# Silu on ScalarE in place of a sigmoid and a product on VectorE, in a two-layer decoder trunk

## The reference

```python
def swiglu(h, w_gate_up, w_down):
    g, u = jnp.split(h @ w_gate_up, 2, axis=-1)
    return (jax.nn.silu(g) * u) @ w_down
# layer 0:  h = h + swiglu(rms_norm(h), ffn_w_gate_up, ffn_w_down)
# layer 1:  out = sum over e of gates[:, e] * swiglu(hn, w_gate_up[e], w_down[e])
```

## Time and profile before

| | before |
|---|---|
| runs | 1892.37, 1892.75, 1894.83 us |
| median | 1892.75 us |
| profiled execution, its span | 1892.9 us |
| TensorE busy | 1694.2 us (90%) |
| VectorE busy | 1352.8 us (71%), 1387 instructions |
| ScalarE busy | 1084.9 us (57%), 1089 instructions |
| mean granted TensorE clock | 0.948 of full speed |
| dense mixer, first activation | 267.87 us after the start |
| ends of the eight turns (last products) | 894.7 to 1831.2 us |

### The profile page before, as it was taken

One profiled execution on the slowest core, in us unless ns is written; L12 is line 12 of the kernel. 1 busy time (PEld: TensorE's weight loads), 2 busy tenths in 40 slices (PEclk: granted clock), 3 DMA queues, 4 the chain that ended last, 5 costly groups with the idle time before them and its releaser, 6 DMA issues.

```text
span 1892.9 us, 21567 instructions
## 1 busy us (share of the span) xinstructions
PE 1694.2 (90%) x7672; PEld 1384.0 (73%) x7672; DVE 1352.8 (71%) x1387; ACT 1084.9 (57%) x1089; POOL 0.2 (0%) x4
## 2 busy tenths in 40 slices
PE   6998889997878686799899999998998998999986
PEld 5885768885658565688787787786886886877865
DVE  6645444555438363798898897897997987988964
ACT  5354333344434342676676676675776766766753
POOL 0000000000000000000000000000000000000000
PEclk9999889998888796899999999999999999999998
DMA  5552334553425104599798897897896996987922
GB/s 223 215 181 86 134 113 177 200 184 127 141 101 185 54 25 187 213 373 347 280 368 316 316 374 306 306 378 285 332 375 255 367 377 244 369 337 293 373 109 89
DMA packets 64077, 459.62 MB, mean 243 GB/s; under 512 B 7200, under 2 KB 7200, under 8 KB 8480
## 3 DMA queue, kind: packets, MB, share of 16 engines
q1 hardware_dynamic: 64032, 459.01, 64.5%
HBM read 457.94 MB, written 1.05 MB: 242 GB/s over the span
## 4 chain that ended last, share of the span: by engine, by line
PE 79%; DVE 11%; ACT 5%; issue 3%; DMA 1%; DVEq 0%; ACTq 0%; SPq 0%
PE banks L366 25%; PE banks L368 24%; PE banks L367 24%; DVE weights_low L1062 3%; ACT weights_high L744 2%; PE banks L439 2%; PE banks L414 1%; DMA raw_static<-static_dram 1%; PE banks L691 1%; PE banks L690 1%; DVE activations_t L1084 1%; DVE residual L1497 1%; ACT activations_t L770 1%; DVE scores_t L1385 0%; PE banks L609 0%
## 5 line engine op out<-in xcount | busy, mean ns | idle before, releaser
L1062 DVE TENSOR_TENSOR weights_low<-scratch,weights_high 128x2048 fp32r<-128x2048 f32 x336 | 761.5, 2289 | 114.8 <-ACT weights_high L744 114.7
L744 ACT ACTIVATE weights_high<-scratch 128x2048 fp32r<-128x2048 f32 x336 | 642.6, 1915 | 124.5 <-PE banks L368 124.4
L366 PE MATMUL banks<-weights_high,activations_t 128*128 128x512 f32 (+1 forms) x1568 | 628.3, 401 | 66.0 <-DVE weights_low L1062 49.8
L367 PE MATMUL banks<-weights_low,activations_t 128*128 128x512 f32 (+1 forms) x1568 | 614.2, 392 | 0.0
L368 PE MATMUL banks<-weights_high,activations_t 128*128 128x512 f32 (+1 forms) x1568 | 614.2, 392 | 0.0
L366 PEld LDWEIGHTS banks<-weights_high,activations_t 128*128 128x128 f32 x1568 | 301.7, 192 | 130.8 <-DVE weights_low L1062 32.4
L368 PEld LDWEIGHTS banks<-weights_high,activations_t 128*128 128x128 f32 x1568 | 301.3, 192 | 62.1
L367 PEld LDWEIGHTS banks<-weights_low,activations_t 128*128 128x128 f32 x1568 | 302.4, 193 | 56.6
L1062 DVE TENSOR_TENSOR weights_low<-raw_static,weights_high 128x2048 fp32r<-128x2048 f32 x99 | 221.8, 2257 | 123.3 <-ACT weights_high L744 121.8
L744 ACT ACTIVATE weights_high<-raw_static 128x2048 fp32r<-128x2048 f32 x99 | 185.1, 1892 | 122.6 <-PE banks L368 110.2
L366 PE MATMUL banks<-weights_high,hidden_t 128*128 128x512 f32 x536 | 214.3, 400 | 9.5 <-DVE hidden_t L1236 9.5
(11 more groups left out here) (226 smaller groups left out, 1026.2 us busy)
## 6 DMA issues: line engine op xcount, KB each, us to landing
scratch<-expert_dram SPq DMA_DIRECT2D x336, 1024.0 KB, 5.5
raw_static<-static_dram SPq DMA_DIRECT2D x97, 1024.0 KB, 4.9
consts_sb<-const_dram SPq DMA_DIRECT2D x1, 1058.0 KB, 6.9
residual<-x_dram SPq DMA_DIRECT2D x1, 1024.0 KB, 4.9
out_dram<-residual SPq DMA_DIRECT2D x2, 512.0 KB, 2.8
small_sb<-small_dram SPq DMA_DIRECT2D x1, 704.0 KB, 8.1
raw_static<-static_dram SPq DMA_DIRECT2D x2, 256.0 KB, 3.0
scratch<-gain_dram SPq DMA_DIRECT2D x1, 512.0 KB, 5.7
```

The costliest lines, as they stand in the source:

```text
L366: pe.matmul(oo, xh, wh, start=first, stop=False)
L367: pe.matmul(oo, xh, wl, start=False, stop=False)
L744: A(WH[:, slot, 0:w], raw[:, 0:w], ACT.Copy).then_inc(high_ready, 1)
L1062: V_.tensor_tensor(WL[:, slot, 0:w], raw[:, 0:w], WH[:, slot, 0:w].bitcast(F32), ALU.subtract).then_inc(low_ready, 1)
```

## The change

In `f_sigmoid` ScalarE evaluates Silu in place of Sigmoid. In `f_hidden` VectorE's first product, the one with the gate columns, is gone together with the wait behind it; the product with the up columns reads `SIG`, which now holds silu(g). The helper `elink` and the semaphore `hid_step` go too, since nothing else uses them. `link` stays for other uses. The name of the function `f_sigmoid` and of its semaphore stay. No slab, bank, DMA or order of other work is touched.

```diff
-        dve_step, hid_step = sem("dve_step"), sem("hid_step")
+        dve_step = sem("dve_step")
...
                 for tt in range(tiles):
-                    m = A(SIG[:, tt, :], gu_bank(n, tt)[:, 0:256], ACT.Sigmoid)
+                    m = A(SIG[:, tt, :], gu_bank(n, tt)[:, 0:256], ACT.Silu)
                 m.then_inc(f_sig, 1)
...
-            def f_hidden(n, fbase, tiles, gu_bank, linked):
+            def f_hidden(n, fbase, tiles, gu_bank):

                 dve.wait_ge(f_sig, fbase + (n + 1))
-                for tt in range(tiles):
-                    m = V_.tensor_tensor(SIG[:, tt, :], SIG[:, tt, :], gu_bank(n, tt)[:, 0:256], ALU.mult)
-                linked(m)
                 for tt in range(tiles):
                     m = V_.tensor_tensor(HID[:, tt, :], SIG[:, tt, :], gu_bank(n, tt)[:, 256:512], ALU.mult)
                 m.then_inc(f_hid, 1)
...
-                f_hidden(n, 0, NT, lambda n, tt: PS[:, 6 + tt, :], link)
+                f_hidden(n, 0, NT, lambda n, tt: PS[:, 6 + tt, :])
...
-                lk = [0]
-
-                def elink(m):
-                    lk[0] += 1
-                    m.then_inc(hid_step, 1)
-                    dve.wait_ge(hid_step, it * ESTEPS + lk[0])
-
...
-                    f_hidden(n, it * ESTEPS + FSTEPS, 1, lambda n, tt: PS[:, 2 + n % 2, :], elink)
+                    f_hidden(n, it * ESTEPS + FSTEPS, 1, lambda n, tt: PS[:, 2 + n % 2, :])
```

## The result

| | before | changed |
|---|---|---|
| runs beside the prediction, median | 1892.56 us (1892.06 to 1894.83, 4) | 1881.98 us (1880.04 to 1884.12, 4) |
| ratio to before | | 0.9937 (0.992 to 0.9954) |
| all unedited executions on record, mean | 1893.7 us (60) | 1882.5 us (13) |
| mean granted clock, where recorded | 0.9483 (56) | 0.9525 (13) |
| profiled execution, its span | 1892.9 us | 1878.5 us |

The change made the kernel 10.6 us faster by the first medians and 11.2 by the means, where 6.7 were forecast. The executions of either kernel scatter over several us (1878.5 to 1885.4 for the changed one), so a pair of profiles is not a measurement: these two differ by 14.4 us.

The account below looks back on a forecast made before the run. TensorE was taken as the bound, busy for 90% of the span, with VectorE's products mattering only where TensorE waits for them. Terms 3.5 + 0.8 + 1.6 + 0.8 = 6.7 us off 1892.75 gave 1886.1 us, range 1882.5 to 1890.5.

Parts of the forecast that it names:

- the clock at the turns' heads: Head of an expert turn: the one clock fall in seven may vanish or move; 0.8 us gained, half of 1.6.
- the stretch behind the dense mixer: From the dense mixer to the experts: the prediction's sum had no term for it, so no gain.
- Turn ends: End of each of eight expert turns: the remaining product starts 0.44 us sooner and all of it counts; 3.5 us gained.
- Dense first step: First dense mixer step: the exposed wait before the second step shrinks from 2.32 to 1.53 us; 0.79 us gained.
- The clock behind the dense stall: Behind the dense mixer's first-step stall: the shorter stall should mostly pass without a clock fall; 1.6 us gained.
- Silu, table loads, the freed time in the steps: Activations and mid-turn steps: Silu takes 385 ns like the sigmoid, table loads stay as many, VectorE's other freed time gains 0.
- slower by the clock: Rival, heads of turns: the 2.08 us stall costs a clock fall in all seven turns; 1898.1 us, chance 0.05.
- more clock than that: Rival, expert turns: two or three of the eight falls behind 2.88 us stalls may vanish too; 1881 to 1883 us, chance 0.10.
- Direct terms only: Rival, whole kernel: clock falls stay as many, only 4.3 us are gained; 1888.4 us, chance 0.20.
- nothing is gained: Rival, turn ends: something arriving no sooner holds the transposes or the next turn's first slab; 1892 us, chance 0.12.
- the two slower ones: Rivals: clock falls at all seven heads, 1898.1 us, chance 0.05; extra table loads in each step, some 1960 us, chance 0.02.

Follow-up runs that it names:

- e3: Changed kernel with a second, serial product back in the last step of each expert only; 1889.0 us, ratio 0.9973 to the kernel before.
- e6: Changed kernel with a second, serial product back in all steps of an expert but the last; 1882.0 us, ratio 0.9932 to the kernel before.
- e2: Kernel before with the change made in the experts only, the dense mixer keeping sigmoid and two products; 1887.31 us, ratio 0.9967.
- e4: Changed kernel with the second pair of products back in the first dense step only; 1886.39 us, ratio 0.9957 to the kernel before.
- e1: Kernel before with the change made in the dense mixer only, the experts keeping sigmoid and two products; 1888.53 us, ratio 0.9978.
- e5: Changed kernel with the second pair of products back in the ten later dense steps; 1884.18 us, ratio 0.9948 to the kernel before.
- e7: Changed kernel with a one-column Silu ahead of the expert loop, loading its table there; 1874.25 us, ratio 0.9901 to the kernel before.
- e0: Changed kernel again, unedited, for more executions; 1882.74 us, ratio 0.9942 to the kernel before.

## Why the prediction was wrong

The direction and the direct terms were right, the sum was too small: 6.7 us against 10.6 to 11.2. Two steps failed: the term for the clock at the turns' heads (4) was too small, and the stretch behind the dense mixer (6) was put at nothing. By its parts:

1. *Turn ends, 8 × 0.44 = 3.5 us.* Right. The 0.46 us wait is gone at each end, the turns are 133.1 us long, and e3 and e6 show that only these eight places count in the experts.
2. *Dense first step, 0.79 us.* Right: 2.32 to 1.53.
3. *The clock behind the dense stall, 1.6 us.* Right in the pair of profiles, too much on average. The 2.32 us stall has its fall in three of the six profiles of before and in none of e2 and e4; behind 1.53 us there is none in twelve profiles. It is worth 0.8 us in the mean, the 1.6 of the table less the direct 0.79.
4. *The clock at the turns' heads, 0.8 us.* This term was mis-sized. I took the single fall of one profile and weighed it by half. The kernel before has 1.5 falls per execution and the changed kernel none: 5.6 − 3.5 = 2.1 us. I took it that a fall may go away or turn up at any other head. The place of the fall behind the residual add shows that the heads are not independent: with two operations at the turn's end it moves by some 0.45 us a turn until a head has its fall, with one it stays (e2, e4 and e6 against e1 and e3). One fall of the 12, in e5, came without such a drift and is unexplained. The rival "slower by the clock" had named what counts, that turns of nearly equal length repeat the same position; here that kept the falls away from the heads. The rule that I had put beside the term, in the Trainium skill, TensorE: Matmul & The Clock Gate (What's actually happening), was that the gate's look runs free of the kernel. The traces agree in that this place differs between executions in the first turn, from 0.4 us ahead of the restart to 1.3 behind it; from there on it follows the program's own times, so the rule was no reason to take half.
5. *Silu, table loads, the freed time in the steps.* Right: 384 ns, 17 loads at the two lines (e7 shows that one load in each turn stands on the path, a cost that both kernels have), and e5 and e6 show that the second operations of the other 114 steps hide (10 dense, 104 in the experts). VectorE's busy time was forecast as 1298 us and is 1311.0, since I took off the products' durations and left out the overlap.
6. *The stretch from the dense mixer to the experts, nothing.* Here the sum failed: I gave the change no term in a stretch whose instructions it leaves alone. It was worth 1.4 us in its first 114 us in the eleven profiles of the two kernels. Over its length up to the experts it was worth 3.7 us (standard error 1.0) by all twenty profiles, and e2 and e4 tie that to the dense stall. The 1.3 us ahead of the dense mixer are scatter: there the eight profiles with the long stall and the twelve with the short one differ by 0.4 us.

Direct 4.3, clock behind the dense stall 0.8, heads 2.1, the stretch behind the dense mixer 3.7: 10.9 us of the 11.2 have a place, to within about 1 us. The halves fit within their intervals: 5.3 us for e1, which measured 4.2 (2.1 to 6.2), and 5.6 for e2, which measured 6.2 (4.2 to 8.3). e4 fits less well: it should have lost the same 5.3 us and lost 2.8, with an uncertainty of about 4. The clock of the whole execution points the same way. At a mean granted clock of 0.9483 and 0.9525, (1 − clock) × span is 97.8 and 89.4 us, 8.4 us less of missing clock, of which some falls on idle time; the direct terms leave 6.9 us for it.

The rival "more clock than that", at 0.10, came nearest by its time, but its place was wrong: the eight stalls behind the residual add keep a fall each in the changed kernel. "Direct terms only" is refuted by e0, e2 and e3, and "nothing is gained" and the two slower ones by the ratio.

A smaller slip was the base. I set the span of 1892.9 us equal to the median of the runs. A run's time lies 1.5 to 1.6 us above its span (1880.12 and 1878.5, 1889.55 and 1888.0), so the profile of before came from an execution of about 1894.5 us. It did not enter the sum, but it should have told me that the executions differ by falls of the clock and that one trace holds a sample of them. The range, 1882.5 to 1890.5, hung on the lower side on that one sample.

## What to carry to other kernels

Look for the places where TensorE waits for the operation that is removed, count them, and leave the rest of its busy time out: here 9 of 123 steps carried all of the direct gain. Then, if the granted clock falls in places, count the stalls that sit near the size at which it sometimes falls, and give the change in falls a term with its own wide bounds, downstream stretches too. Before sizing such a term from one trace, compare the profiled execution's time with the spread of the runs. And read what stands in series at a loop's head: a table load there can be taken out by one activation ahead of the loop.

## What the runs showed of the hardware that was not expected

- A stall shortened by 0.79 us changed how long TensorE's clock was at its lower level (1.2 GHz) in a stretch over 200 us later: 0.83 of full speed over 30 us in all eight profiles with the longer stall, 0.89 in all twelve with the shorter one.
- The same stall of 2.32 us was followed by a fall of the clock in three of eight executions, one of 1.53 us in none of twelve; stalls of 2.06 to 2.13 us at the heads in 11 of 56 with one length of turn and in 1 of 63 with another that is 0.44 us shorter. Stalls of 2.87 us behind the residual add had one in every turn of both kernels, but in e7, with shorter turns, two of eight had none.
- In a loop with turns of 133.55 us the place of the clock's fall moved by 0.45 us a turn against TensorE's restart, in one with turns of 133.1 us it stayed.
- The two table loads per turn (1283 ns each) are there because the loop can be entered with another table; with Silu's table loaded on both ways in, there was none in any turn.
- A VectorE instruction that does not wait overlaps the end of the one before it by 0.08 us; taking out 134 products took 55.1 us off the durations but 41.8 us off the busy time, since fewer neighbours overlap.
